# Two block sums of a feed-forward weight, made by copying and accumulating DMAs in DRAM instead of on GpSimd

## The reference

```
h = rms_norm_2(x, norm_mlp)
return x + jnp.square(jax.nn.relu(h @ w_ff1)) @ w_ff2
```

## Time and profile before

| what | value |
|---|---|
| median of 3 runs | 1040.5 us (1040.49 to 1040.62) |
| span of the profiled execution | 1039.7 us |
| PE busy | 1028.8 us, 99 % |
| PE weight load busy | 844.4 us, 81 % |
| DVE busy | 656.1 us, 63 % |
| ACT busy | 536.3 us, 52 % |
| POOL busy | 350.2 us, 34 % |
| DMA | 146.24 MB, mean 141 GB/s |
| of it q1 (SP's DMAs) | 129.70 MB |
| of it q10 (ACT's DMAs) | 12.88 MB |
| of it q0 (POOL's DMAs) | 2.75 MB |
| granted TensorE clock | 9 (of tenths) in each of 40 slices of the span |

### The profile page before, as it was taken

One profiled execution on the slowest core, in us unless ns is written; L12 is line 12 of the kernel. 1 busy time (PEld: TensorE's weight loads), 2 busy tenths in 40 slices (PEclk: granted clock), 3 DMA queues, 4 the chain that ended last, 5 costly groups with the idle time before them and its releaser, 6 DMA issues. The chain is left out here.

```text
span 1039.7 us, 14348 instructions
## 1 busy us (share of the span) xinstructions
PE 1028.8 (99%) x5310; PEld 844.4 (81%) x5310; DVE 656.1 (63%) x1141; ACT 536.3 (52%) x960; POOL 350.2 (34%) x334
## 2 busy tenths in 40 slices
PE   9999999999999999999999999999999999999997
PEld 7788878888878898878887788888888888888885
DVE  5578998675765346823577888343222325999976
ACT  8454345454672355544667874224343346554554
POOL 0022010003330002900354510008779945653542
PEclk9999999999999999999999999999999999999999
DMA  9655332313320384132200551248999942443542
GB/s 333 117 112 122 89 94 63 81 49 135 134 92 1 103 265 142 46 92 71 61 1 2 177 189 46 76 164 300 355 349 343 321 151 64 149 145 129 203 183 81
DMA packets 99637, 146.24 MB, mean 141 GB/s; under 512 B 6208, under 2 KB 60224, under 8 KB 99568
## 3 DMA queue, kind: packets, MB, share of 16 engines
q1 hardware_dynamic: 86016, 129.70, 38.0%
q10 hardware_dynamic: 12768, 12.88, 4.0%
q0 software_dynamic: 784, 2.75, 1.8%
HBM read 123.69 MB, written 21.63 MB: 140 GB/s over the span
## 5 line engine op out<-in xcount | busy, mean ns | idle before, releaser
L2462 DVE TENSOR_TENSOR w_lo<-wring,w_hi 128x1024 fp32r<-128x1024 f32 x32 | 48.2, 1505 | 114.2 <-ACT w_hi L1846 114.2
L1992 DVE TENSOR_TENSOR u_lo<-wring,u_hi 128x1024 fp32r<-128x1024 f32 (+1 forms) x64 | 80.8, 1272 | 51.2 <-ACT u_hi L1540 50.7
L869 PE MATMUL bank<-u_hi,h_hi 128*128 128x512 f32 (+1 forms) x288 | 110.9, 385 | 0.1
L869 PE MATMUL bank<-u_hi,h_lo 128*128 128x512 f32 (+1 forms) x288 | 109.2, 379 | 0.0
L869 PE MATMUL bank<-u_lo,h_hi 128*128 128x512 f32 (+1 forms) x288 | 109.0, 378 | 0.0
L1540 ACT ACTIVATE u_hi<-wring 128x1024 fp32r<-128x1024 f32 (+1 forms) x64 | 65.9, 1033 | 79.0 <-PE bank L869 57.5
L869 PE MATMUL bank<-h_hi,w_lo 128*128 128x512 f32 (+2 forms) x272 | 104.5, 384 | 0.0
L869 PE MATMUL bank<-h_hi,w_hi 128*128 128x512 f32 (+2 forms) x272 | 104.4, 384 | 0.0
L869 PE MATMUL bank<-h_lo,w_hi 128*128 128x512 f32 (+2 forms) x272 | 104.3, 384 | 0.0
L869 PE MATMUL bank<-h_hi,u_hi 128*128 128x512 f32 x224 | 94.1, 420 | 0.3 <-ACT arena L1482 0.2
L1370 PE MATMUL bank<-s_hi,f_hi 128*128 128x512 f32 x224 | 88.5, 395 | 0.1
(11 more groups left out here) (374 smaller groups left out, 2496.8 us busy)
## 6 DMA issues: line engine op xcount, KB each, us to landing
wring<-in_w_in SPq DMA_DIRECT2D x60, 512.0 KB, 3.9
wring<-in_w_ff ACTq DMA_DIRECT2D x12, 1024.0 KB, 8.8
wring<-sums_kept SPq DMA_DIRECT2D x16, 768.0 KB, 4.2
wring<-in_w_ff SPq DMA_DIRECT2D x22, 512.0 KB, 6.2
wring<-in_w_ff SPq DMA_DIRECT2D x32, 256.0 KB, 3.3
sums_kept<-wring SPq DMA_DIRECT2D x22, 256.0 KB, 4.9
arena<-in_w_out SPq DMA_DIRECT2D x4, 1024.0 KB, 5.1
wring<-in_w_out SPq DMA_DIRECT2D x2, 2048.0 KB, 12.8
```

Source lines behind the costliest of these rows:

```text
L869: last = mm(b, lhs, rhs, start=(start and n == 0), stop=(stop and n == 2))
L1992: v.tensor_tensor(u_lo[u % RAW_UNITS][:, 0:cols], raw_unit(u), u_hi[u % HI_UNITS][:, 0:cols].bitcast(F32), ALU.subtract).then_inc(u_lo_don ...
L2462: v.tensor_tensor(cut(w_lo[ring3(m)]), src, cut(w_hi[ring3(m)]).bitcast(F32), ALU.subtract).then_inc(w_lo_done, 1)
```

## The change

Of the four sums of a pair, POOL goes on making the two differences, from the same loads. The two plain sums are made in DRAM. In its stream, between the last `scale_heads` and the combos, POOL issues eight DMAs that copy blocks of `w_ff2` to `sums_kept[:, :, 0:1024]` (b11 for the first half, b22 for the second, four pairs and 1.05 MB each), and, when the copies have landed and the masks are made, eight DMAs of the same shape with `accum_op=add`, which add b12 or b21 to what lies there. SP waits for these (`rows_added`) before it reads for the second product. The thresholds of `w_summed` and `sums_out` are lowered to the smaller number of sums and writes. Two semaphores of fills (`ones_done`, `zeroed`) become one (`filled_done`), and the semaphores `vec_out` and `strips_b_in` are used a second time to count the copies.

```diff
+        def w2_rows(half, q, side):
+            rows = w["w_ff2_2"].rearrange("(j n p) d -> n j p d", n=2, p=P)[half]
+            return rows[4 * q:4 * q + 4, :, S * side:S * (side + 1)]
+
+        def kept_rows(half, q):
+            return sums_kept[4 * q:4 * q + 4, :, S * half:S * (half + 1)]
...
+        copied, copied_from = [vec_out, strips_b_in], (16, 16 * P // COPIES)
+        rows_added = sem("rows_added")
...
-                    sp.wait_ge(sums_out[(j - 3) % 2], 48 * ((j - 3) // 2 + 1))
+                    sp.wait_ge(sums_out[(j - 3) % 2], 32 * ((j - 3) // 2 + 1))
...
             def keep_sums(j):
-                sp.wait_ge(w_summed, 4 * j + 4)
+                sp.wait_ge(w_summed, 2 * j + 2)
                 lower, upper = sum_raw[j % 3]
-                sp.dma_start(sums_kept[j][:, 0:D], sum_out[j % 2]).then_inc(sums_out[j % 2], 16)
...
             for n in range(2):
-                sp.wait_ge(sums_out[n], 48 * NP // 2)
+                sp.wait_ge(sums_out[n], 32 * NP // 2)
+            sp.wait_ge(rows_added, 128)
...
                 if m < NP:
-                    act.wait_ge(w_summed, 4 * NP + m + 1)
+                    act.wait_ge(w_summed, 2 * NP + m + 1)
...
             scale_heads("ka")
             scale_heads("qa")
+            pool.wait_ge(strips_b_in, 16 * P // COPIES)
+            for half in range(2):
+                for q in range(4):
+                    pool.dma_start(kept_rows(half, q), w2_rows(half, q, half)).then_inc(copied[half], 16)
             pool.wait_ge(masks_done, NT - 1)
+            for half in range(2):
+                pool.wait_ge(copied[half], copied_from[half] + 64)
+                for q in range(4):
+                    pool.dma_start(kept_rows(half, q), w2_rows(half, q, 1 - half), accum_op=ALU.add).then_inc(rows_added, 16)
             for c, t in enumerate(combos):
...
             def pair_sums(j):
                 pool.wait_ge(sum_in[j % 3], (16, 16, 0)[j % 3] + 32 * (j // 3 + 1))
-                if j >= 2:
-                    pool.wait_ge(sums_out[j % 2], 48 * (j // 2))
                 (b11, b12), (b21, b22) = ((a[:, 0:S], a[:, S:D]) for a in sum_raw[j % 3])
-                g.tensor_tensor(sum_out[j % 2][:, 0:S], b11, b12, ALU.add).then_inc(w_summed, 1)
-                g.tensor_tensor(sum_out[j % 2][:, S:D], b21, b22, ALU.add).then_inc(w_summed, 1)
-                pool.wait_ge(w_summed, 4 * j + 1)
                 g.tensor_tensor(b12, b12, b22, ALU.subtract).then_inc(w_summed, 1)
-                pool.wait_ge(w_summed, 4 * j + 2)
                 g.tensor_tensor(b21, b21, b11, ALU.subtract).then_inc(w_summed, 1)
```

More of the change, by code:

```diff
@@ L476, in f1_cols @@
             return w["w_ff1_2"][:, 2 * P * h:2 * P * (h + 1)].rearrange("(k p) n -> p k n", p=P)
-        sum_out = [wring[:, 12288:12288 + D], arena[:, 26720:26720 + D]]
+        def w2_rows(half, q, side):
[3 more added lines that the diff above has]
+            return sums_kept[4 * q:4 * q + 4, :, S * half:S * (half + 1)]
         ff_pair = lambda j: ffT[:, 2 * j:2 * j + 2, :].rearrange("p c s -> p (c s)")
@@ L522, in build @@
         first_lo_done = sem("first_lo_done")
-        ones_done = sem("ones_done")
+        filled_done = sem("filled_done")
         rs_done = sem("rs_done")
@@ L576, in build @@
         kc_lo_done = sem("kc_lo_done")
-        zeroed = sem("zeroed")
         rope_done = sem("rope_done")
@@ L757, in _ @@
                         if u == U2 + 5:
-                            sp.wait_ge(zeroed, 1)
+                            sp.wait_ge(filled_done, 2)
                             for m, a in enumerate(("cmp_k_w2_2", "cmp_v_w2_2")):
@@ L933, in fill @@
                     t_unit(name, e, [k])
-            pe.wait_ge(ones_done, 1)
+            pe.wait_ge(filled_done, 1)
             for _ in range(12):
@@ L1741, in _ @@
                 if kind == "hidk":
-                    act.wait_ge(zeroed, 1)
+                    act.wait_ge(filled_done, 2)
                 if tile == ("ga", 7):
@@ L2572, in _ @@
             g = nc.gpsimd
-            g.memset(ones, 1.0).then_inc(ones_done, 1)
+            g.memset(ones, 1.0).then_inc(filled_done, 1)
             pool.wait_ge(vec_done, 1)
@@ L2626, in _ @@
                 g.memset(z, 0.0)
-            g.memset(vdiag, 0.0).then_inc(zeroed, 1)
+            g.memset(vdiag, 0.0).then_inc(filled_done, 1)
             chain = [0]
```

## The result

The changed kernel takes 1097.5 us (1097.4 to 1098.6, four runs) against 1040.6 us of the kernel before (1040.5 to 1040.6, four runs). The ratio is 1.0547, with a 95 % interval of 1.0535 to 1.056. The direction is the forecast one, the size is not: 1055 us was forecast, with a range up to 1078.

What follows compares the result with a forecast made beforehand. PE was taken to bound the kernel. On the 1039.7 us span, 0 (removed) + 0 (POOL) + 14.8 (late loads) gave 1054.5 us, forecast as a 1055 us median; main case 1043 to 1071, 8-in-10 range 1040.0 to 1078.

Steps and rivals of the forecast that it cites:

- What bounds the kernel: Whole kernel: PE works 1028.8 of 1039.7 us, so nothing off PE is worth more than about 3.5 us.
- What is removed: First feed-forward product: POOL's 57 us of sums, SP's 8.39 MB of writes; counted 0, bounded by 0 and -3.5 us.
- The traffic's size: DMA queues from about 160 us: copies 31 us (20 to 87), adds at least as long, at most twice.
- The rival on few engines: First attention: one copy lies on only four engines and delays loads, loss of 16 to 45 us; chance 0.14.
- How late a load is: First attention's w_in loads: each of 64 packets per engine stands behind one of POOL's, 7.7 us late.
- the prediction's own slacks: First attention: lateness the five w_in loads can bear, 2.9, 6.2, 6.3, 5.4 and 2.9 us.
- The term forecast at 14.8 us: First attention: lateness of 7.7 us less slack, summed over the five w_in loads, 14.8 us.
- POOL's issues: POOL ahead of the combos: issuing eight DMAs costs 4.6 to 18.4 us, with time until about 235 us; counted 0.
- The rival "POOL comes late": First attention: copies landing at 247 us make the third combo up to 30 us late, 1071 us; chance 0.05.

## Why the prediction was wrong, step by step

**What bounds the kernel: right.** PE does, with no idle time to give back.

**What is removed, counted at 0: right,** shown alone by two runs (0.9996 and 0.9999) and in the changed kernel by the unchanged beat.

**The traffic's size: right as engine time, wrong as duration.** The copies were put at 31 us on all 16 engines, and took 453 / 16 = 28 us; the adds at 31 to 62 us, and took 869 / 16 = 54 us. The copies' figure came out in part by luck: there are 128 packets with data for each engine, at 0.18 us, where 256 at 0.121 us were counted, and 5 us more are packets of 8 bytes. But the adds of the change lasted from 182 us to 320 us (the last, issued at 288 us, landed 32.4 us later), and up to 292 us POOL's queue had only 54.5 % of the engines. The traffic was expected to end at 222 us, at 253 with two reads. That they would not fill the engines was not considered. The rival on few engines, with 0.14, had the reason right, four engines for a transfer, as the quarter of 272 to 286 us shows; but it used it only for the lateness of a load.

**How late a load is: right in its form, with too cheap a packet.** 7.7 us were taken, 5.1 and 10.9 were the bounds. The five loads landed after 17.9, 13.6, 17.5, 15.9 and 18.3 us, so 13.9, 9.6, 13.5, 11.9 and 14.3 us late, 12.6 us on average. The count of one packet for one packet is borne out for three of the five. While the first load was under way, from 163.3 to 181.2 us, the trace has this of all queues and of POOL's:

```profile
DMA packets 5701, 5.30 MB, mean 296 GB/s; under 512 B 2700, under 2 KB 4658, under 8 KB 5700
...
q0 software_dynamic: 3712, 4.29, 76.9%
```

Most of POOL's packets are the ones of 8 bytes, 0.01 us each. With data there are 1042, of 4 KB: 65 for each engine, against the load's 64. For the third and the fifth load it is 61 and 69. The term that was mis-sized is the price: 0.121 us, for a packet taken as one row of 2 KB. The copies' packets are of 4 KB and took 0.187 us here, the adds' of 2 KB 0.18 us, and 64 of these are 11.5 to 12.0 us, above the bound of 10.9. The second and the fourth load met fewer, 43 and 35 for each engine on the mean, and were 9.6 and 11.9 us late all the same; that the traffic was heavier on some engines than on others would explain it, but is not shown.

With the measured lateness the prediction's own slacks would have given 11.0 + 3.4 + 7.2 + 6.5 + 11.4 = 39.5 us; measured were 25.5 us, since a stall moves the later loads' users along and so gives them slack (behind the second and the fourth load PE did not wait). The term forecast at 14.8 us measured 25.5.

**POOL's issues: wrong, and this is the step that decided.** "Eight cost 4.6 to 18.4 us" priced the writing of an issue and no more. POOL stood another 92.3 us in them and came to the combos at 289 us, where 235 was the limit. The earlier waits had moved that limit too, to 271 us, when DVE began to stand: 19.2 us of PE wait, that the sum had at 0. The rival "POOL comes late" had the right victim and threshold, with 0.05, but another reason (copies that land after 217 us). The same stay, moved to another place, cost 49 us, and with the rows outermost, in the run of 1065.2 us, it was gone.

**The clock: missing.** PE's matmuls take 12.0 us more in all, at the lower granted clock after each wait. No row of before had shown PE waiting long enough for that, and the sum charged each microsecond of wait once.

The sum now closes by the trace: 25.5 (loads) + 19.2 (combos) = 44.7 us of new waits, less 0.8 us of idle time elsewhere, + 12.0 us of slower matmuls = 55.9 us, the difference of the two spans. Against the forecast 14.8 us, 10.7 are missing in the loads' term, 19.2 in POOL's and 12.0 in the clock's.

**What stays open.** What is full when POOL's issue blocks: in the four-pairs shape seven copies went out at once and the eighth stood 16.6 us, of the adds at most three went out together, while in the other shape eight DMAs went out at once. The stays end with a landing, but what the landing sets free was not measured. Nor is it settled why the sixteen-engine shape delays the branch loads at 604 us so much more than the other one.

## What to carry to other kernels

A DMA that is issued from an engine's stream is not free for that engine: it may stand in the issue until an earlier transfer has landed, and then what stands behind it in that stream is late, so put such blocks where nobody waits for what follows. Traffic is cheap or dear by its neighbours: the same 16.8 MB in the same shape cost 24 us beside weight loads with 3 to 6 us of slack and 2 us in a stretch without urgent loads. The order of a transfer's dimensions is part of the design: in the same place it made 57 us or 24. And before work is moved off an engine that is not the bound, leave it out altogether once: here that would have told that there was nothing to win.

## What the runs showed of the hardware

- POOL stood up to 28.2 us (29.8 us behind the second attention) in one DMA issue with no semaphore to wait for; the four stays ahead of the change's adds ended 0.2 to 0.4 us after an earlier transfer had landed. SP's issue of a load, 0.4 us otherwise, took up to 6.95 us while the DMA engines were full (a share of 1.02).
- One accumulating DMA of 1 MB from DRAM to DRAM, alone in flight, with 4 as its outermost dimension on both sides: a DMA share of 0.28 and 52 GB/s. With 128 outermost: 1.13 and 207 GB/s.
- A load of 512 KB in rows of 512 bytes took 4.0 us alone and 13.6 to 18.3 us beside this traffic. It passed 61 to 69 packets for each engine, of 2 to 4 KB at 0.18 us, for 64 of its own, in three cases of five.
- Two orders of the same dimensions of a DRAM-to-DRAM transfer of 1 MB differed by 32 us in the whole kernel, 1097.5 against 1065.2 us, for the better; elsewhere by 21 us for the worse.
- Accumulating DMAs took 1.92 times the engine time of copies of the same bytes, in twice as many packets of half the size, at the same 0.18 us for each.
- After a PE wait of 10 us the granted clock was 0.50 for some 4 us and back at 1.00 within 8 us.
